# The indirect gather of the next item's tokens, moved behind the indirect add of the last item's rows

## What is computed

```python
logits = jnp.einsum('ld,de->le', h, w_router) + b_router
top_val, top_idx = lax.top_k(logits, TOP_K)              # 4 of 32
gates = jax.nn.softmax(top_val, axis=-1)
flat_e = top_idx.reshape(-1); order = jnp.argsort(flat_e)
tok = order // TOP_K
xs = h[tok]                                              # rows of the tokens, by expert
hgu = lax.ragged_dot(xs, w_gate_up, group_sizes) + b_gate_up[e_sorted]
act = _clamped_swiglu(hgu)
out = lax.ragged_dot(act, w_down, group_sizes) + b_down[e_sorted]
out = out * gates.reshape(-1)[order][:, None]
return jax.ops.segment_sum(out, tok, num_segments=L)     # added up by token
```

## Time and profile before

| | |
|---|---|
| median of 3 runs | 1970.95 us (1967.66 to 1971.95) |
| the profiled execution | 1965.19 us, of which the span from first to last instruction is 1963.4 us |
| granted TensorE clock, mean | 0.976 |
| TensorE matmul busy | 1859.5 us, 95% |
| VectorE busy | 1647.7 us, 84% |
| ScalarE busy | 1357.9 us, 69% |
| GpSimd busy | 455.4 us, 23% |
| DMA | 526.22 MB, mean 268 GB/s over the span |
| the scatter (L839) | 50 instructions, 2162 ns each on average |
| the gather (L805) | 33 in `item_rows` and 2 before it |

### The profile page before, as it was taken

The page is one execution under the profiler, slowest core; times in us unless marked ns, Lnnn a source line. Parts: engine busy times, 40 slices in busy tenths (PEclk is TensorE's granted clock), DMA queues, the critical chain, the costliest instruction groups (busy, mean ns, idle before and its releaser), DMA issues.

```text
span 1963.4 us, 28736 instructions
## 1 busy us (share of the span) xinstructions
PE 1859.5 (95%) x8464; PEld 1450.4 (74%) x8464; DVE 1647.7 (84%) x1766; ACT 1357.9 (69%) x1777; POOL 455.4 (23%) x412
## 2 busy tenths in 40 slices
PE   6999999998989999999999999999999999999897
PEld 3657767787758887877777787677777778777775
DVE  6899987349765478989999998898898999989897
ACT  4556855224345525888788887888888888888885
POOL 6671000000000116412312311321222222212122
PEclk7999999999999998999999999999999999999999
DMA  8222225422110248999999999999999999999995
GB/s 321 81 107 86 86 79 190 138 83 91 34 43 23 47 155 266 355 376 377 368 403 375 373 376 381 366 367 387 368 363 404 374 383 375 391 383 358 399 380 209
DMA packets 134432, 526.22 MB, mean 268 GB/s; under 512 B 15809, under 2 KB 21089, under 8 KB 114208
## 3 DMA queue, kind: packets, MB, share of 16 engines
q1 hardware_dynamic: 118704, 492.45, 66.5%
q0 software_dynamic: 15664, 32.97, 6.5%
HBM read 512.76 MB, written 23.74 MB: 273 GB/s over the span
## 4 chain that ended last, share of the span: by engine, by line
PE 30%; DMA 12%; DVE 7%; ACT 5%; issue 5%; SPq 0%; ACTq 0%; DVEq 0%
PE ps L1135 25%; DMA ring<-in_w_gate_up 8%; DVE split L2826 4%; DMA arena<-in_w_gate_up 3%; PE ps L1184 3%; DVE arena_r L2826 2%; ACT arena_r L2024 2%; ACT split L2024 2%; ACT arena L2049 1%; PE ps L1088 1%; PE ps L1174 1%; DMA arena<-in_w_down 1%; DMA ring<-in_w_down 1%; DVE aTs L2770 0%; ACT arena L2060 0%
## 5 line engine op out<-in xcount | busy, mean ns | idle before, releaser
L1135 PE MATMUL ps<-split,xTs 128*128 128x512 f32 x2016 | 509.9, 401 | 20.3 <-DVE split L2826 14.7
L1135 PEld LDWEIGHTS ps<-split,xTs 128*128 128x128 f32 x2016 | 379.4, 191 | 120.3 <-DVE split L2826 33.4
L2826 DVE TENSOR_TENSOR split<-ring,split 128x2048 fp32r<-128x2048 f32 x136 | 308.2, 2295 | 42.6 <-ACT split L2024 36.9
L2826 DVE TENSOR_TENSOR split<-arena,split 128x2048 fp32r<-128x2048 f32 x136 | 308.7, 2286 | 4.0 <-ACT split L2024 3.6
L2024 ACT ACTIVATE split<-ring 128x1024 fp32r<-128x1024 f32 x272 | 272.5, 1057 | 51.4 <-DMA ring<-in_w_gate_up 47.3
L2024 ACT ACTIVATE split<-arena 128x1024 fp32r<-128x1024 f32 x272 | 272.5, 1052 | 44.8 <-DMA arena<-in_w_gate_up 16.1
L839 POOL DMA_INDIRECT y_rows<-arena,slots x50 | 108.1, 2162 | 336.4 <-issue 299.0
L1135 PE MATMUL ps<-arena_r,xTs 128*128 128x512 f32 x672 | 182.1, 405 | 0.9 <-DVE arena_r L2826 0.4
L1135 PE MATMUL ps<-arena_r,aTs 128*128 128x512 f32 x672 | 170.3, 398 | 0.0
L1135 PE MATMUL ps<-split,aTs 128*128 128x512 f32 x672 | 168.2, 396 | 1.0 <-DVE aTs L2886 0.3
L2826 DVE TENSOR_TENSOR arena_r<-ring,arena_r 128x2048 fp32r<-128x2048 f32 x68 | 157.1, 2311 | 3.6 <-ACT arena_r L2024 3.6
(11 more groups left out here) (480 smaller groups left out, 3128.1 us busy)
## 6 DMA issues: line engine op xcount, KB each, us to landing
ring<-in_w_gate_up SPq DMA_DIRECT2D x170, 1024.0 KB
arena<-in_w_gate_up SPq DMA_DIRECT2D x102, 1024.0 KB
arena<-in_w_down SPq DMA_DIRECT2D x102, 1024.0 KB
ring<-in_w_down SPq DMA_DIRECT2D x34, 1024.0 KB
ring<-in_w_in SPq DMA_DIRECT2D x23, 1024.0 KB
ring<-in_w_out SPq DMA_DIRECT2D x8, 1024.0 KB
ring<-in_mod_w SPq DMA_DIRECT2D x10, 512.0 KB, 9.2
ring<-in_mod_w SPq DMA_DIRECT2D x4, 1024.0 KB
```

Of the source, the lines that this page charges most:

```text
L1135: m = mm(ps[:, banks + q, :], lhs[:, x_, k, :], w[:, q * 512:(q + 1) * 512], start=start, stop=stop)
L2826: V.tensor_tensor(split_pair(1, p), chunk_pair(p), split_pair(0, p), ALU.subtract).then_inc(sig("lo_ready"), 1)
```

## The change

In `item_rows` the gather no longer stands ahead of the wait for `y_ready`, but behind the scatter. With two scatters it stands between them. Nothing is added or taken away.

```diff
--- before.py
+++ after.py
@@ -850,14 +850,12 @@
                 m = it.i
                 wait_alone(pool, sig("xt_ps"), pool.to_reg(m * 2 + 2))
                 wait_alone(pool, sig("slot_g_in"), pool.to_reg(m * 16))
+                wait_alone(pool, sig("y_ready"), pool.to_reg(m + 0))
+                scatter(0, HALF_SLOTS if before_small else P)
                 gather(idx_g[0:HALF_SLOTS, :] if it.next_small else idx_g)
-                wait_alone(pool, sig("y_ready"), pool.to_reg(m + 0))
                 if before_small:
-                    scatter(0, HALF_SLOTS)
                     wait_alone(pool, sig("scattered"), pool.to_reg(it.rows - 16))
                     scatter(HALF_SLOTS, P)
-                else:
-                    scatter(0, P)
                 wait_alone(pool, sig("gathered"), pool.to_reg(m * 16 + 32))
                 if it.small:
                     load_slots(slot_g[0:HALF_SLOTS, :], m + 2, HALF_SLOTS, sig("slot_g_in"))
```

## The result

| | before | with the change |
|---|---|---|
| median of runs beside each other | 1967.30 us (20 runs) | 1976.18 us (20 runs, 1969.27 to 1992.93) |
| ratio | 1 | **1.0056, 95% interval 1.0042 to 1.0071** |
| profiled execution, its span | 1965.19, 1963.4 us | 1983.05, 1981.4 us |

The change costs 11.0 us (0.0056 x 1967.3), 8.3 to 14.0; the forecast was +19.9. The ratio rests on all 20 runs of each kernel; the two medians alone are 8.9 us apart. From here on "+9 us" means 9 us behind the output copy that opens an item, and the ratios are all against the kernel before.

A forecast was written before the change was run, and what follows sets the result against it. Small items were taken to wait for weights, big ones for TensorE. Small items' gather +17.9 and item 1 +2.0, the rest 0, sum to +19.9 us: 1990.9 against the median; range 1962 to 2002, the forecast's own 1973 to 2002.

The forecast's parts named there:

- term 2: 64-row gather in big items, moved between the two scatters: 0, bounds -0.3 and +0.3 us per item.
- Term 1: 128-row gather in small items 2 to 28, moved into the stretch short of weights: 14 x 1.28 = +17.9 us.
- The yardstick: Small item 14, whose gather was late before the change: +1.84 us, less 0.56 for an earlier tile, gives 1.28.
- The bound of 2.0 us: Upper end per small item: 128 rows of 4 KB, 0.52 MB at 3.87 us per MB of all 16 engines.
- my own first paragraph: Small items wait for weights, big ones for TensorE; slack just ahead of the small item, shortage in its first 20 us.
- Term 3, item 1: In item 1 gather and scatter change places back to back; gather starts 2.6 us later: +2.0 us (1.6 to 2.4), once.
- Term 3, the new wait elsewhere: Gather now behind `y_ready`; in item 8 it lands 8.8 us ahead of TensorE's need: cost 0.
- The rival had this as a uniform delay of all items: TensorE waits for gathered rows in every small item; at 2 us each, 14 x 2 = +28 on top; chance 0.03.
- The rule of the Trainium skill on taking turns: Engines alternate between queue rows, so the late gather passes queued weights: 14 x 2.0 = 28 us, time 2001.
- Faster: Rival: gather leaves the way of small items' first tiles, half the 2.04 us wait goes: -12, 1959 us; chance 0.20.
- The clock: Rival: more idle time brings four more small items with lowered clock, +9.3, so +29 in all: 2000 us; chance 0.13.
- The tail: Last slot load has 2.5 us of room for a scatter landing about 1 us later: 0, bounds 0 and +1.

## Why the prediction was right and wrong

The direction was right, slower, and the time lies in the range; the size was not: +19.9 forecast, +11.0 measured, and the interval ends at 14.0. Nearly two thirds of the miss of 8.9 us are term 2.

- **Term 1, the 128-row gather in small items, +17.9: right in size, wrong in its picture.** 15.9 by the difference of two kernels (about 12 to 20), 1.14 us each for 1.28. The yardstick, item 14 of the kernel before, needed no theory of the slack and was good. ScalarE's longest wait for `ring` was to come at 3 us or more and is 3.54 in item 12, but that wait is long since the first tile came some 3 us sooner; the relief of an earlier tile is there as well (the first ring tile goes from +9.4 to +9.0 with the small items' order, 0.4 us; I had taken 0.56). The picture was that the gather leaves slack ahead of the item. Only its instruction stood there: its packets run from about -1 to +3 (79 rows in item 8), and it goes from one part of the item's first 16 us to another. What it costs is the rate of 301 GB/s from +4 to +8. The bound of 2.0 us counted 128 full rows. That small items would rise from 34.2 to 35.5 was wrong (those at full clock took 31.7 to 34.1 us), as was reading them by themselves: the big items' order shortens them and lengthens the big ones at the same time.
- **Term 2, the 64-row gather in big items, 0 with bounds of 0.3 per item: the step that failed.** It is -5.7 us, -0.41 per item, beyond the bound. I asked only what the gather meets in its new place (nothing, as the run without it shows) and not what it left: its old place "about 8 us ahead of the output copy" is the end of the small item, which by my own first paragraph waits for weights (I had put the shortage in its first 20 us alone). There its packets lowered the rate from 387 to 334 GB/s, and with it gone the pairs of items are shorter. The same edit was costed by its arrival in one kind of item and should have been by departure and arrival in both.
- **Term 3, item 1, +2.0: +0.7.** The gather started at 811.10, as worked out, and landed sooner than forecast:

```profile
820.07 1.09 PE L1086 MATMUL ps<-const,arena 128*128 128x128 f32 x8 [0.69 <-DMA arena<-h_rows,slots]
```

- **Term 3, the new wait elsewhere, 0:** right in the undisturbed item (in item 12 the gather starts at 1183.20, the slot load behind it at 1196.49, TensorE's transposes without a wait at 1203.57) and wrong as a rule without exceptions. GpSimd is late now and then, by list work behind a drawn-out scatter, and the margin that the old order had is gone. The rival had this as a uniform delay of all items, at 0.03; it came in single items, 9.5 us in one item of one profile and 7.9 us over three items in another. Moving the list work took 0.0018 from the changed kernel and 0.0014 from the one before, so the list work makes about nothing of the difference; what the drawn-out scatters make of it in the median stays open.
- **The rule of the Trainium skill on taking turns** (DMA: Bandwidth & Descriptors, Queues, rings and completion order), which gave 2001 us in the prediction. The late gather's price, 1.6 us each, is near the 2.0 that was taken from it, and q0 and the weights do share the engines while the gather's packets run. But the early gather shares them too, so the rule tells no difference of the two places, and the difference came mostly ahead of the packets.
- **Faster:** this rival's condition was met. The first ring tile comes ahead of the gather's packets, 2.7 us sooner, and its wait is gone. But the second tile gained only 0.4 us, and TensorE's lack of weights behind it decided, as the prediction had held against the rival.
- **The clock:** items 8 and 28 had 0.86 and took 37.0 us each, and item 14 had 0.84; the lowest before were items 2 and 28 with 0.90. In either profile seven of the small items 2 to 30 were below 1.00, and TensorE took 3.3 us more for the same matmuls. The rival's 9 us were not needed to explain the time; the runs do not separate it.
- **The tail:** no sign of it either way, nor was it tried alone.

With term 2 at -5.7 and item 1 at 0.7, the forecast's own sum would have been 17.9 - 5.7 + 0.7 = 12.9, within the interval. That term 1 came out so near is in part luck, since the 15.9 us hold waits that it did not count.

## What to carry to other kernels

Cost a moved transfer twice, where it goes and where it comes from, and ask of both places which engine waits there. The place of a transfer is where its packets run and not where its instruction stands, here 6 us apart: look at its queue by window. Take a transfer away before you read a dip in GB/s as its work or as slack for it; here one dip was there without the gather, one was the scatter's and one was the gather's. When one edit runs in two kinds of stages, try each kind alone first; here half of the change was worth keeping, and the whole was not.

## What the hardware showed

- An indirect gather of 0.36 MB on average, issued 4.3 us into an item that waits for weights, lowers what the 16 busy DMA engines move from 374 (no gather) to 301 GB/s for the next 4 us, ahead of nearly all of its own packets. Half of its rows do no less: 313 GB/s there, and 326 for 423 still from +12 to +16. The Trainium skill (DMA: Bandwidth & Descriptors, The descriptor swizzle) gives, for a transfer over 128 partitions, a formula by which the engine follows from the partition: partitions 0 to 63 fall to engines 0 to 7. If that held for 64 rows too, half of the rows would load half of the engines as much as before; no row here shows single engines.
- GpSimd's small operations on lists, 0.24 us with no subtraction of VectorE beside them, take as long as one whole subtraction when one runs: 2.2 us, or 1.1 with the subtraction halved. The Trainium skill (SBUF — State Buffer, Who interferes with whom) says that a VectorE instruction with two SBUF inputs contends with a GpSimd instruction that reads SBUF; these rows agree. The same section infers that such an instruction leaves the making of DMA descriptors alone; the scatter instructions of 11.6 and 13.6 us beside just these subtractions speak against it, without proving it wrong.
- Two stores of 32 single 4-byte words each cost an item 5 to 7 us: the DMA engines move 94 GB/s in the worst 4 us beside them.
